# Gated product of an FFN step transposed by VectorE and 16 SBUF transfers in place of TensorE

## The reference

```python
def swiglu(x, w_in, w_out):
    gu = x @ w_in                      # 1024 -> 2 * 2816
    g, u = jnp.split(gu, 2, axis=-1)
    return (jax.nn.silu(g) * u) @ w_out  # 2816 -> 1024

x = x + 0.5 * swiglu(rms_norm(x, ffn1_norm[l]), ffn1_w_in[l], ffn1_w_out[l])   # first block, twice a layer
x = x + (jax.nn.silu(gate) * up) @ w_down[l]                                   # second block
```

## Time and profile before

| | |
|---|---|
| time, median of 3 runs | 1720.64 us (1720.05 to 1723.21) |
| span of the profiled execution, first to last instruction | 1721.5 us |
| TensorE busy with matmuls | 1671.8 us, 97% |
| VectorE busy | 943.5 us, 55% |
| ScalarE busy | 803.8 us, 47% |
| mean granted clock of TensorE, of full speed | 0.990 |
| DMA | 308.96 MB, 179 GB/s on average |

### The profile page before, as it was taken

How to read it: one execution, slowest core, us unless ns; L and a number is a source line. 1 busy time by engine, 2 the same in 40 slices (tenths; PEclk the granted TensorE clock), 3 DMA queues, 4 the chain that set the end, 5 groups by cost and what they waited for, 6 DMA issues and landing times.

```text
span 1721.5 us, 22066 instructions
## 1 busy us (share of the span) xinstructions
PE 1671.8 (97%) x7760; PEld 1376.7 (80%) x7760; DVE 943.5 (55%) x843; ACT 803.8 (47%) x899; POOL 97.1 (6%) x105
## 2 busy tenths in 40 slices
PE   6999999999999999999999999899999999999998
PEld 5887887888888787888888888787888878788886
DVE  4545545575545645465566545566554556665454
ACT  5443454544434543444455444465444446544443
POOL 2010000010000002000001000021100002110000
PEclk9999999999999999999999999999999999899999
DMA  8875453446565578555345655644456564336552
GB/s 259 295 221 175 172 190 123 139 156 199 176 208 188 175 251 240 174 173 181 111 152 166 203 188 194 240 127 129 141 190 200 179 195 144 125 127 201 189 192 89
DMA packets 209187, 308.96 MB, mean 179 GB/s; under 512 B 10400, under 2 KB 153504, under 8 KB 208480
## 3 DMA queue, kind: packets, MB, share of 16 engines
q1 hardware_dynamic: 208272, 305.18, 54.1%
q0 software_dynamic: 560, 1.84, 0.4%
q10 hardware_dynamic: 288, 1.05, 0.2%
HBM read 306.97 MB, written 2.88 MB: 180 GB/s over the span
## 4 chain that ended last, share of the span: by engine, by line
PE 90%; DVE 3%; ACT 3%; issue 2%; DMA 1%; POOL 1%; DVEq 0%; SPq 0%; ACTq 0%; POOLq 0%
PE pg L1380 19%; PE pg L1381 18%; PE pg L1382 18%; PE acc L1382 9%; PE acc L1380 9%; PE acc L1381 9%; PE pg L1451 2%; DVE wlo L970 2%; ACT whi L671 1%; DMA raw<-in_ffn_w_in 1%; PE pg L1393 1%; PE acc L1530 1%; PE acc L1550 1%; POOL ms L590 0%; PE acc L1538 0%
## 5 line engine op out<-in xcount | busy, mean ns | idle before, releaser
L970 DVE TENSOR_TENSOR wlo<-raw,whi 128x2048 fp32r<-128x2048 f32 x277 | 641.2, 2316 | 513.8 <-ACT whi L671 513.8
L671 ACT ACTIVATE whi<-raw 128x2048 fp32r<-128x2048 f32 x277 | 529.5, 1913 | 338.6 <-PE pg L1382 168.2
L1380 PE MATMUL pg<-whi,xTh 128*128 128x512 f32 (+1 forms) x1456 | 580.3, 399 | 9.9 <-DVE wlo L970 5.7
L1382 PE MATMUL pg<-whi,xTl 128*128 128x512 f32 (+1 forms) x1456 | 570.4, 392 | 0.0
L1381 PE MATMUL pg<-wlo,xTh 128*128 128x512 f32 (+1 forms) x1456 | 570.2, 392 | 0.0
L1380 PEld LDWEIGHTS pg<-whi,xTh 128*128 128x128 f32 x1456 | 276.3, 190 | 73.6 <-DVE wlo L970 9.8
L1382 PEld LDWEIGHTS pg<-whi,xTl 128*128 128x128 f32 x1456 | 276.0, 190 | 57.5
L1381 PEld LDWEIGHTS pg<-wlo,xTh 128*128 128x128 f32 x1456 | 276.5, 190 | 54.3
L1380 PE MATMUL acc<-whi,bTh 128*128 128x512 f32 (+1 forms) x572 | 229.6, 401 | 0.0
L1382 PE MATMUL acc<-whi,bTl 128*128 128x512 f32 (+1 forms) x572 | 224.3, 392 | 0.0
L1381 PE MATMUL acc<-wlo,bTh 128*128 128x512 f32 (+1 forms) x572 | 223.1, 390 | 0.0
(11 more groups left out here) (159 smaller groups left out, 1048.2 us busy)
## 6 DMA issues: line engine op xcount, KB each, us to landing
raw<-in_ffn_w_in SPq DMA_DIRECT2D x176, 512.0 KB, 4.8
raw<-in_ffn_w_out SPq DMA_DIRECT2D x88, 512.0 KB, 4.0
raw<-in_w_gate_up SPq DMA_DIRECT2D x88, 512.0 KB, 4.7
raw<-in_mix_w_in SPq DMA_DIRECT2D x64, 512.0 KB, 4.1
raw<-in_w_down SPq DMA_DIRECT2D x44, 512.0 KB, 4.0
raw<-in_w_in SPq DMA_DIRECT2D x24, 512.0 KB, 4.8
raw<-in_mix_w_o SPq DMA_DIRECT2D x16, 512.0 KB, 4.7
raw<-in_w_o SPq DMA_DIRECT2D x16, 512.0 KB, 4.5
```

The lines of the kernel that those rows point to most:

```text
L671: act_e.activation(whi[:, slot, :], raw[:, slot, :], ACT.Copy).then_inc(s.w_hi_ready, 1)
L970: v.tensor_tensor(wlo[:, slot, :], raw[:, slot, :], f32(whi[:, slot, :]), ALU.subtract).then_inc(s.w_lo_ready, 1)
L1380: pe.matmul(dst, xh, wh, start=first and i == 0, stop=False)
L1382: mm = pe.matmul(dst, xl, wh, start=False, stop=last and i == len(pairs) - 1)
```

## The change

In nine of the eleven steps of each FFN (products of steps 1 to 9; 54 of 66 in all) TensorE's `turn` is gone. In its place:

- VectorE transposes `act` in blocks of 32 x 32 into `turned` with one instruction (new line 1071), after the product of t = 1 and before its refill of slot 0.
- SyncE moves the blocks to where they belong in a transposed matrix with 16 transfers, each 32 partitions x 128 numbers, 16 KB, SBUF to SBUF (`move`, new line 500). They stand between its load of slot 2 and its load of slot 0; the first waits for VectorE's transpose and for the low part of the product before.
- ScalarE's high part and VectorE's low part read `moved` in SBUF instead of the PSUM bank; ScalarE waits for all 16 transfers (`moved_hi`, `moved_lo`).

The products of steps 0 and 10 are transposed by TensorE as before. Inside `bTh` and `bTl` the order of the 128 x 128 squares is another; it costs no instruction.

```diff
+                def move(j):
+                    sp.wait_ge(s.act_turned, TURNED * f + j)
+                    sp.wait_ge(s.actT_lo, STEPS * f + j)
+                    for a in range(QUADS):
+                        for b in range(QUADS):
+                            sp.dma_start(moved_blocks[Q * b:Q * (b + 1), a, :], turned_blocks[Q * a:Q * (a + 1), b, :])\
+                                .then_inc(s.act_moved, 16)
...
-                        gate_up((2, 0), (rnd + j, rnd + j + 1), j + 1)
+                        gate_up((2, 0), (rnd + j, rnd + j + 1), j + 1, (lambda: move(j - 1)) if begin >= 2 else None)
                         down(1, rnd + j + 1, j)
                 down(2, rnd + STEPS - 1, STEPS - 1)
+                move(STEPS - 2)
...
+                def moved_hi(j, par):
+                    act_e.wait_ge(s.act_moved, 16 * MOVES * (TURNED * f + j))
+                    act_e.activation(actTh[:, par].rearrange("p n (a i) -> p n a i", a=QUADS), moved_T,
                                      ACT.Copy).then_inc(s.actT_hi, 1)
...
+                def step(j, par, turn=True):
+                    refill(1, rnd + j + 1)
+                    product(0, 1 - par, j + 1)
+                    refill(2, rnd + j + 1)
+                    product(1, 1 - par, j + 1)
+                    if turn:
+                        v.wait_ge(s.act_ready, 2 * STEPS * f + 2 * j + 4)
+                        v.transpose(turned_blocks, act_blocks).then_inc(s.act_turned, 1)
+                    refill(0, rnd + j + 2)
...
                         for k in range(2):
                             for n2 in range(2):
                                 mm = added(t, par, slot, n2, k, first and k == 0, False)
-                        if t == 0:
-                            turn(j + 1, 1 - par)
+                        if t == 0 and last:
+                            turn(STEPS - 1, 0)
```

More of the change, by code:

```diff
@@ L1014, in ffn, with product_lo, moved_lo @@
                 product(1, 0, 0)
-                def product_lo(j, par):
+                def product_lo(j, src):
                     v.wait_ge(s.actT_hi, STEPS * f + j + 1)
[L1018 to L1030, removed]
-                product_lo(STEPS - 1, 0)
+                    v.tensor_tensor(actTl[:, 0], src[:, :].rearrange("p (n i) -> p n i", n=TT * 2), f32(actTh[:, 0]),
+                                    ALU.subtract).then_inc(s.actT_lo, 1)
+                def moved_lo(j, par):
+                    v.wait_ge(s.actT_hi, STEPS * f + j + 1)
+                    hi, lo = (b[:, par].rearrange("p n (a i) -> p n a i", a=QUADS) for b in (actTh, actTl))
+                    v.tensor_tensor(lo, moved_T, f32(hi), ALU.subtract).then_inc(s.actT_lo, 1)
+                def step(j, par, turn=True):
+                    refill(1, rnd + j + 1)
+                    product(0, 1 - par, j + 1)
+                    refill(2, rnd + j + 1)
+                    product(1, 1 - par, j + 1)
+                    if turn:
+                        v.wait_ge(s.act_ready, 2 * STEPS * f + 2 * j + 4)
+                        v.transpose(turned_blocks, act_blocks).then_inc(s.act_turned, 1)
+                    refill(0, rnd + j + 2)
+                product_lo(0, pg[0][0])
+                step(0, 0)
+                with v.Fori(0, (STEPS - 3) // 2) as jj:
+                    for par in (1, 0):
+                        j = 2 * jj + 2 - par
+                        moved_lo(j, par)
+                        step(j, par)
+                moved_lo(STEPS - 2, 1)
+                step(STEPS - 2, 1, False)
+                product_lo(STEPS - 1, pg[0][0])
                 def add(t, n2):
@@ L1450, in turn, with down @@
                         for c in range(2):
[L1451 removed]
+                            tr = pe.transpose(pg[par][0][:, (2 * t + c) * P:(2 * t + c + 1) * P], act[:, t, c * P:(c + 1) * P], ident[:, :])
                     tr.then_inc(s.actT_tr, 1)
                 def added(t, par, slot, n2, k, first, last):
[L1455 removed]
+                    return product(acc[2 * t + n2][:, :], [(actTh[:, par, 2 * t + k, :], actTl[:, par, 2 * t + k, :],
                                                             *weights(slot, k * D + n2 * BANK, BANK))], first=first, last=last)
[L1458 removed]
+                def down(j, par, slot, r, first, last):
                     pe.wait_ge(s.actT_lo, STEPS * f + j + 1)
@@ L1484, in last_down, with step @@
                                     transposes(0, n2, o + 1)
-                def step(j, par, amid=None, first=False):
+                def step(j, par, amid=None, first=False, last=False):
                     full_block((2, 0), (rnd + j, rnd + j + 1), BANK, pg[1 - par], s.ffn_t0_done, amid=amid)
-                    down(j, par, 1, rnd + j + 1, first)
+                    down(j, par, 1, rnd + j + 1, first, last)
                 step(0, 0, {(0, 1): lambda: turn(0, 0)}, first=True)
@@ L1493, in ffn @@
                     step(2 * jj + 2, 0)
-                step(STEPS - 2, 1)
+                step(STEPS - 2, 1, last=True)
                 last_down(2, rnd + STEPS - 1)
```

64 lines of the change are left out of this document (39 added, 25 removed).

## The result

| | before | changed |
|---|---|---|
| time, median | 1721.24 us (1720.05 to 1723.21, 4 runs) | 1939.72 us (1934.81 to 1942.94, 4 runs) |
| span of the profiled execution | 1721.5 us | 1933.0 us |
| TensorE busy with matmuls | 1671.8 us, 97% | 1731.7 us, 90% |
| mean granted clock | 0.990 | 0.944 |

The ratio is 1.1263, 95% interval 1.1249 to 1.1276: 218 us slower. The forecast was 1890 (own range 1850 to 1965), 50 us too low: 41 of it in the span, 5 because the profiled run is the quickest of the four, the rest from rounding and the step between span and time.

A forecast was written before the change was run, and what follows sets the result against it. TensorE bounds the kernel at 16.79 us a step; the change makes a 20.05 us loop outside TensorE the bound, 28.5 us more per FFN, 171 in six: 1890 us, own range 1850 to 1965, 8 in 10 1700 to 1965.

The forecast's parts named there:

- TensorE's share, 25.4 us: Four transposes removed from TensorE in each moved step: 54 times 0.47 us, leaving a step of 16.32 if all else hides.
- The loop: Path through VectorE, SyncE, transfers and ScalarE that closes once a step without TensorE; its length is 10.9 + 15x us.
- P: Length of that once-a-step path from one VectorE refill of slot 2 to the next: 20.05 us with issues 0.61 apart.
- The block transpose: VectorE's new instruction after the product of t = 1: 0.69 us and 0.05 to start, taken from a same-size row.
- x: Spacing of SyncE's sixteen issues: 0.56 + 0.05 = 0.61 us, ends 0.38 and 0.80, break-even 0.40.
- narrow transfers: Reason for the issue price: full 128 partitions are issued cheaply, others dearly, read from 64-partition loads at 0.60 us.
- Cheap issue: Rival on SyncE's queue: 32 partitions issue like 128, spacing 0.38, 1705 us, floor 1695 below 0.36; chance 0.20.
- Dearer issue: Rival on SyncE's queue: spacing from 0.71, as GpSimd's; at 0.80 the time is 2045 us; chance 0.05.
- The clock: Rival on TensorE: waits slow its matmuls; a third slow loses nothing, all 72 slow gives 2142 us; chance 0.03.
- The sum: `down(9)` starts at 97.2 + 135x = 179.6 instead of 151.1: 28.5 us later per FFN, 171 in six.
- The rest of the FFN is as before: Assumption that after `down(9)` starts, nothing else in the FFN changes its time.
- transfers that land long after 2 us because they queue behind the 1 MB loads: Sign listed as showing the forecast wrong, on SyncE's queue; issue to landing was taken as 2.1 us.

The follow-up runs named there:

- Experiment 1: Changed kernel without its 16 transfers; high and low part read the block transpose's output directly (computation altered): 1693.42 us, ratio 0.9829.
- Experiment 5: Changed kernel with the high and low part placed behind silu and product of t = 0, not ahead of the refill of slot 1: 1808.26 us, ratio 1.0496.
- Experiment 2: Changed kernel with the same bytes in 8 transfers of 32 x 256 instead of 16, blocks not put in their right places: 1745.91 us, ratio 1.0132.
- experiment 3: Changed kernel with sixteen 16 KB transfers each over 128 partitions x 32 numbers, straight across, instead of 32 x 128: 1947.49 us, ratio 1.1301.
- experiment 4: Kernel before, plus groups of eight small transfers behind its end, varying partitions and memories; ran once: issues 0.59 to 0.60 us SBUF to SBUF.
- experiment 9: Changed kernel with the attention bias's four loads singly ahead of steps 5 to 8 of each first FFN, not together ahead of step 6: 1926.94 us, ratio 1.1182.
- experiment 6: Changed kernel with its 16 transfers split, eight issued by SyncE and eight by ScalarE's queue: 1766.53 us, ratio 1.0259.
- experiment 7: Changed kernel with high and low part taken one operation later and eight transfers on each of SyncE's and ScalarE's queues: 1722.54 us, ratio 1.0006.

## Why the prediction was right, and by how much it missed

- *TensorE's share, 25.4 us.* Right, and a little small. Experiment 1 has the step at the 16.32 worked out, and 1693.4 against 1696. The step that I read was 16.79, while most of the kernel before are 16.82, so a turn costs 0.50: 27 us in all. The kernel before also loses 4.7 and 2.3 us in the first FFN of each layer, where a refill of VectorE takes 6.13 us instead of 2.29 beside GpSimd's pass over the attention's bias (the kernel before, ahead of the wait of the earlier trace rows):

```profile
125.93 6.13 DVE L970 TENSOR_TENSOR wlo<-raw,whi 128x2048 fp32r<-128x2048 f32 x1 [3.68 <-ACT whi L671]
```

  In experiment 1 that step of 19.4 is followed by one of 13.4, and nothing is lost. Against these 34 us stand 4 by which its stage boundaries are longer, which leaves the 30 by which its span is shorter.
- *The loop.* Right in every term: refill, product, transpose, sixteen issues, landing, high part, refill. That P came out at 20.05 against 20.11 is in part luck: the first issue is 0.15 later than forecast and the fifteen pitches 0.3 longer, and the landing, 1.8 from SBUF to SBUF where I took 2.1 from loads out of HBM, gives 0.3 back. Experiment 5 shows that what stands behind the wait belongs to its length: the same transfers with the wait one operation later give 17.51. Experiment 2 gives the other limit: eight issues in the same place and the quiet steps are TensorE's.
- *The block transpose.* 0.71 against 0.69.
- *x.* The pitch is (10.02 - 0.59) / 15 = 0.63 against 0.61, of it 0.59 the issue and 0.04 the gap. The number held by luck, and its reason did not hold. I had put 0.60 down to narrow transfers; experiments 3 and 4 show that it is both ends in SBUF, at any width. Had the changed kernel gone through DRAM with 32 partitions, my reason would have given 0.56 where 0.42 is measured.
- *The rivals.* Cheap issue: the groups of experiment 4 with an end in DRAM, at 0.42, come near it, but this kernel's transfers have none. Dearer issue: no. The Trainium skill ("DMA: Bandwidth & Descriptors", section "Issuing engines are not separate DMA queues") has the time to initiate as usually small against the transfer; for these it is 0.59 beside 1.8 to landing, and sixteen in a row take 10.0, so the trace disagrees with it here.
- *The clock.* Right that nothing is lost. TensorE waits 1.99 us; behind that the granted clock is 0.54 over 3.7 us (1.2 GHz for most of it, matmuls 0.43 apart), then 1.00 again. The forecast's idle time of 3.7 shows as 2.0 of waiting and 1.7 of slow matmuls (nine take 3.75 us, 1793.48 to 1797.23, where 9 x 0.2267 is 2.04), and `down` does not come later for it.
- *The sum.* 6 x 28.5 = 171 was 198 in the FFNs and some 211 in all; the forecast came within a quarter of the change because the quiet steps are most of it. What failed is the sentence "The rest of the FFN is as before" and the counting of 54 equal steps. It missed two terms. One: in the first FFN of each layer SyncE also loads gains and biases, and blocks issued behind such a heap wait for it: 173.3 instead of 161.4 for nine transposes, 12 us each, of which the kernel before had itself lost 4.7 and 2.3; experiment 9, which takes the attention's heap apart, gets 7 to 13 us back. Two: at the end of an FFN the first loads of the next stage stand behind the last sixteen transfers. Of the 5.6 and 8.5 us at two boundaries, 1.8 and 6.9 are theirs by experiment 1; the other 5 are there without any transfer. The prediction had listed "transfers that land long after 2 us because they queue behind the 1 MB loads" as what would make it wrong, but priced it at nothing.

What stays open: the gate's heap was not taken apart alone (its step is 22.9 in experiment 9 as before), and the late first loads of a stage were not moved forward, so the second term is read from the traces only. Why two boundaries are longer by 3.7 and 1.6 us without any transfer stays open as well.

## What to carry to other kernels

A chain of small transfers is priced by count times issue time, plus one landing, and it has to be followed around the in-order queue that waits for it. Both ends pay: halving the issues of the queue gave 173 us (experiment 6), taking the wait one operation later 131 (experiment 5), both together 217 (experiment 7). Once data of the inner loop goes through a load queue, every other load in that queue is on its path: look at the steps that load something extra and at the ends of stages before multiplying a quiet step by the number of steps. Taking a small piece of work (0.5 us a step here) from the bounding engine pays only if the detour stays below the slack everywhere.

## What the runs showed of the hardware

- The issue of a DMA by SyncE: 0.59 to 0.60 us from SBUF to SBUF with 32 or 128 partitions, 0.42 to 0.43 with one end in DRAM and 32 or 128 partitions (the first of a row 0.34 to 0.35), 0.60 for 64 partitions from DRAM. ScalarE's queue: 0.61, and the two issue at the same time without slowing each other's issues (eight take 5.0 us on either).
- From issue to landing of 16 KB from SBUF to SBUF: 1.8 us, as a median of the sixteen in a row too; 3.8 when two queues issue eight each (experiment 6); 9.9 at most in the changed kernel, and 9.7 in the row behind the bias loads shown above.
- VectorE's transpose in blocks, 128 x 512 of fp32: 0.711 us, as long as an ordinary pass over the same numbers.
- VectorE's subtraction of 128 x 512 took 2.26 and 2.42 us instead of 0.69 when it met GpSimd's pass over 128 x 4096 (8.8 us long), and that of 128 x 2048 6.13 instead of 2.29 in the kernel before.
- A wait of TensorE of 1.99 us was followed by a granted clock of 0.54 over 3.7 us (nearly all at 1.2 GHz); behind the waits of three other steps of the same FFN, 1.85 to 2.40 us, it was 0.57 to 0.62.
